# A gated linear recurrence with its key-times-query scores on the diagonal computed once for both directions, and matmul chunks of two projections moved

## The reference, cut to what matters

```
def hgrn2_mixer(h, w_in, lb, gn_g, w_out):
    q, z_f, z_b, v, g = jnp.split(h @ w_in, 5, axis=-1)
    q = jax.nn.silu(q.astype(jnp.float32))
    ...
    # q2, v2, z2: 8 heads forward and the same 8 heads with time reversed
    logf = jnp.logaddexp(jnp.log(lb_h), jnp.log1p(-lb_h) + jax.nn.log_sigmoid(z2))
    k2 = (1 - lb_h) * jax.nn.sigmoid(-z2)
    out = _chunk_scan(q2, logf, k2, v2)
    o = out[:, :, 0] + out[:, ::-1, 1]
    o = o * lax.rsqrt(jnp.mean(o * o, axis=-1, keepdims=True) + EPS)
    o = o * gn_g.astype(jnp.float32).reshape(HGRN_HEADS, HGRN_DV)
    o = o.reshape(b_sz, s_len, D_MODEL).astype(h.dtype) * jax.nn.silu(g)
    return o @ w_out
# in _chunk_scan, bcum being the running sum of logf in a chunk:
#   scores[t, s] = sum_k q[t, k] * exp(bcum[t, k] - bcum[s, k]) * k[s, k]   for s <= t
#   o = (q * exp(bcum)) @ state + scores @ v
```

## Time and profile before

| | us |
|---|---|
| median of 3 runs | 2232.5 (2225.56 to 2234.05) |
| the profiled execution | 2231.72 |
| its span | 2229.9 |
| PE busy | 2108.7 (95%) |
| DVE busy | 1484.1 (67%) |
| ACT busy | 917.9 (41%) |

### The profile page before, as it was taken

The page is one execution under the profiler, slowest core; times in us unless marked ns, Lnnn a source line. Parts: engine busy times, 40 slices in busy tenths (PEclk is TensorE's granted clock), DMA queues, the critical chain, the costliest instruction groups (busy, mean ns, idle before and its releaser), DMA issues.

```text
span 2229.9 us, 26958 instructions
## 1 busy us (share of the span) xinstructions
PE 2108.7 (95%) x10048; PEld 1637.4 (73%) x10048; DVE 1484.1 (67%) x2641; ACT 917.9 (41%) x1737; POOL 15.5 (1%) x15
## 2 busy tenths in 40 slices
PE   4888999999998999999999999999999989999998
PEld 2665567777666776577888887788888777888886
DVE  6567775667365599977565555899999965343433
ACT  3344453344443342344233233665666634232231
POOL 1000000000000000000000000000000000000000
PEclk8999998999998999999999999999999999999999
DMA  8422222343223221134555551111111112232321
GB/s 327 170 97 73 88 71 71 132 143 114 95 92 105 68 67 48 38 133 151 180 191 177 186 187 61 57 58 50 55 49 56 48 50 82 86 104 95 94 95 57
DMA packets 65985, 228.77 MB, mean 103 GB/s; under 512 B 7105, under 2 KB 9281, under 8 KB 65729
## 3 DMA queue, kind: packets, MB, share of 16 engines
q1 hardware_dynamic: 65856, 227.05, 30.6%
HBM read 224.93 MB, written 2.10 MB: 102 GB/s over the span
## 4 chain that ended last, share of the span: by engine, by line
PE 78%; DVE 14%; ACT 4%; issue 3%; DMA 1%; SPq 0%; DVEq 0%; ACTq 0%
PE bank L377 20%; PE bank L379 20%; PE bank L378 20%; DVE arena L1737 6%; PE bank L1999 4%; PE bank L649 2%; PE bank L683 1%; PE bank L1188 1%; PE bank L1213 1%; DVE w_lo L315 1%; PE bank L2036 1%; PE bank L1202 1%; DVE arena L497 1%; ACT arena L1231 1%; PE bank L933 1%
## 5 line engine op out<-in xcount | busy, mean ns | idle before, releaser
L377 PE MATMUL bank<-h_hi,w_hi 128*128 128x512 f32 (+1 forms) x1616 | 666.0, 412 | 24.8 <-DVE h_lo L643 13.2
L379 PE MATMUL bank<-h_hi,w_lo 128*128 128x512 f32 (+1 forms) x1616 | 638.3, 395 | 0.0
L378 PE MATMUL bank<-h_lo,w_hi 128*128 128x512 f32 (+1 forms) x1616 | 636.1, 394 | 0.0
L306 ACT ACTIVATE w_hi<-w_raw 128x1024 fp32r<-128x1024 f32 (+3 forms) x293 | 290.9, 994 | 300.0 <-PE bank L379 289.5
L315 DVE TENSOR_TENSOR w_lo<-w_raw,w_hi 128x1024 fp32r<-128x1024 f32 (+3 forms) x290 | 332.8, 1149 | 88.4 <-ACT w_hi L306 88.0
L377 PEld LDWEIGHTS bank<-h_hi,w_hi 128*128 128x128 f32 (+1 forms) x1616 | 307.8, 190 | 99.6 <-issue 28.7
L379 PEld LDWEIGHTS bank<-h_hi,w_lo 128*128 128x128 f32 (+1 forms) x1616 | 306.5, 190 | 68.6
L378 PEld LDWEIGHTS bank<-h_lo,w_hi 128*128 128x128 f32 (+1 forms) x1616 | 308.0, 191 | 61.2 <-issue 4.1
L377 PE MATMUL bank<-a_hi_t,w_hi 128*128 128x512 f32 x512 | 203.0, 396 | 0.0
L378 PE MATMUL bank<-a_lo_t,w_hi 128*128 128x512 f32 x512 | 203.0, 396 | 0.0
L379 PE MATMUL bank<-a_hi_t,w_lo 128*128 128x512 f32 x512 | 202.9, 396 | 0.0
(11 more groups left out here) (254 smaller groups left out, 2475.0 us busy)
## 6 DMA issues: line engine op xcount, KB each, us to landing
w_raw<-weights_dram SPq DMA_DIRECT2D x261, 512.0 KB, 3.6
ada_raw<-ada_dram SPq DMA_DIRECT2D x128, 512.0 KB, 3.6
arena<-ada_dram SPq DMA_DIRECT2D x8, 1024.0 KB, 15.8
w_raw<-weights_dram SPq DMA_DIRECT2D x16, 256.0 KB, 2.6
xT<-x_dram SPq DMA_DIRECT2D x1, 2048.0 KB, 14.4
out_dram<-xT SPq DMA_DIRECT2D x8, 256.0 KB, 2.2
tables<-tables_dram SPq DMA_DIRECT2D x1, 1536.0 KB, 19.8
w_raw<-weights_dram SPq DMA_DIRECT2D x8, 144.0 KB, 3.5
```

What stands on the lines that cost most here:

```text
L306: nc.scalar.activation(WH[:, slot, 0:w], RAW[:, raw, 0:w], ACT.Copy).then_inc(w_hi_ready, 1)
L377: nc.tensor.matmul(o, WH[:, slot, cols], self.hi(k), start=(k == 0), stop=False)
L378: nc.tensor.matmul(o, WH[:, slot, cols], self.lo(k), start=False, stop=False)
L379: last = nc.tensor.matmul(o, WL[:, slot, cols], self.hi(k), start=False, stop=(k == self.K - 1))
```

## The change

It does five things.

1. Own scores are shared: DVE adds the keys of both directions (`add_keys`, into `KK`) once per head, PE computes one own score per head, and DVE keeps its diagonal once. `A` is not begun anew for direction 1, and `pv_own` runs once per head, after both directions. So a head has 15 scores and not 16, and its counts of `pv` are 3 and not 4.
2. The score of level 64 (p = 1) is computed only where it is needed: 64 keys by 64 queries of each token tile, and DVE moves it by a plain copy of 64 partitions by 4x64.
3. The other levels' `pick` copies only the half of each block pair that the level can fill, 256 and not 512 elements per partition, still through the mask.
4. Unit 0 takes 4 of its 10 parts of the next projection in slot 0, ahead of the first cross product; each other slot has 1 part.
5. The output projection has three tiles in its chunk-by-chunk opening. Chunks 0 to 6 of the third are put into `HgrnEnd`: two behind `pv_own`, five behind `sum_pe`.

Besides, `R` takes the place of `SQ`, and the second norm's steps are renumbered for a projection with one step less.

```diff
             def score_pe(self, pe, u, p):
-                e = 8 * u + p
+                e, d = self.event(u, p), u % 2
                 if e >= 2:
                     pe.wait_ge(self.picked.sem, self.picked.at(e - 1))
                 if p == 0:
-                    pe.wait_ge(self.k_made.sem, self.k_made.at(u + 1))
+                    pe.wait_ge(self.k_added.sem, self.k_added.at(u // 2 + 1))
...
+                    if p == 1:
+                        keys, queries = 64 * d, 64 - 64 * d
+                        last = nc.tensor.matmul(bank[4 + e % 2][keys:keys + 64, j * P + queries:j * P + queries + 64], lhs[:, j * P + keys:j * P + keys + 64],
+                                                rhs[:, j * P + queries:j * P + queries + 64], start=True, stop=True)
...
+            def add_keys(self, dve, h):
...
+                nc.vector.tensor_tensor(self.KK, K[:, 0, :], K[:, 1, :], ALU.add).then_inc(self.k_added.sem, 1)
...
+                if p == 1:
+                    keys, queries = slice(64 * d, 64 * d + 64), slice(64 - 64 * d, 128 - 64 * d)
+                    nc.vector.tensor_copy(A3[keys, :, queries], b3[keys, :, queries]).then_inc(self.picked.sem, 1)
                 else:
...
+                    half = slice(m, 2 * m) if d == 0 else slice(0, m)
...
+                    nc.vector.copy_predicated(A4, mask.unsqueeze(1).to_broadcast([P, NT, P // (2 * m), m]), b4).then_inc(self.picked.sem, 1)
...
+                self.parts = self.PARTS if u else (4, 1, 1, 1, 1, 1, 1)
...
                 if l == 0:
-                    self.part(pe, 0)
-                    if u:
-                        H.pv_own(pe, u - 1)
-                    H.score_pe(pe, u, 0)
+                    for i in range(self.parts[0]):
+                        self.part(pe, i)
+                    if u == 0:
+                        H.cross_pe(pe, 0)
+                    if d == 0:
+                        if h:
+                            H.pv_own(pe, h - 1)
+                        H.score_pe(pe, u, 0)
                     H.score_pe(pe, u, 1)
...
             def pe(self, pe):
-                self.H.pv_own(pe, 15)
+                self.H.pv_own(pe, 7)
+                for k in range(2):
+                    self.project.chunk(pe, k, (2,))
                 self.H.sum_pe(pe, 7)
+                for k in range(2, 7):
+                    self.project.chunk(pe, k, (2,))
...
-            weave((pr, 2, 1), (gains, 2.1, 1), (n2, 3.2, 0.2, 0, 2), (n2, 4.2, 1, 2, 8), (n2, 10.3, 1, 8, 9))
+            weave((pr, 2, 1), (gains, 2.1, 1), (n2, 3.2, 0.2, 0, 3), (n2, 4.2, 1, 3, 8), (n2, 9.3, 1, 8, 9))
```

More of the change, by code:

```diff
@@ L1993, in score_pe @@
                     pe.wait_ge(self.ready.sem, self.ready.at(g + 1))
[L1994 removed]
+                    lhs = rhs = self.X[:, g % 2, :]
                 for j in range(NT):
                     c = slice(j * P, (j + 1) * P)
[L1997 to L1999 removed]
+                    if p == 1:
+                        keys, queries = 64 * d, 64 - 64 * d
+                        last = nc.tensor.matmul(bank[4 + e % 2][keys:keys + 64, j * P + queries:j * P + queries + 64], lhs[:, j * P + keys:j * P + keys + 64],
+                                                rhs[:, j * P + queries:j * P + queries + 64], start=True, stop=True)
+                    else:
+                        last = nc.tensor.matmul(bank[4 + e % 2][:, c], lhs[:, c], rhs[:, c], start=True, stop=True)
                 last.then_inc(self.scored.sem, 1)
             def pick(self, dve, u, p):
[L2003 removed]
+                e, d = self.event(u, p), u % 2
                 dve.wait_ge(self.scored.sem, self.scored.at(e + 1))
@@ L2038, in pv_cross, with pv_own @@
                 last.then_inc(self.pv.sem, 1)
-            def pv_own(self, pe, u):
-                h = u // 2
-                pe.wait_ge(self.picked.sem, self.picked.at(8 * u + 8))
-                for r in range(NT):
-                    last = nc.tensor.matmul(bank[6 + h % 2][:, self.tile(u, r)], self.VT[:, self.order(u, r), :], self.A[:, self.tile(u, r)],
-                                            start=False, stop=True, skip_group_check=True)
+            def pv_own(self, pe, h):
+                pe.wait_ge(self.picked.sem, self.picked.at(15 * h + 15))
+                for j in range(NT):
+                    c = slice(j * P, (j + 1) * P)
+                    last = nc.tensor.matmul(bank[6 + h % 2][:, c], self.VT[:, j, :], self.A[:, c], start=False, stop=True, skip_group_check=True)
                 last.then_inc(self.pv.sem, 1)
             def square_act(self, act, h):
-                act.wait_ge(self.pv.sem, self.pv.at(4 * h + 4))
+                act.wait_ge(self.pv.sem, self.pv.at(3 * h + 3))
                 if h:
-                    act.wait_ge(self.summed.sem, self.summed.at(h))
+                    act.wait_ge(self.applied.sem, self.applied.at(2 * h - 1))
                 nc.scalar.activation(self.SQ, bank[6 + h % 2][:], ACT.Square).then_inc(self.squared.sem, 1)
@@ L2088, in build, with chunk @@
         class Begun(Project):
-            def chunk(self, pe, k):
-                for t in range(self.outer):
+            def chunk(self, pe, k, tiles=(0, 1)):
+                for t in tiles:
                     if k == 0:
@@ L2102, in first_tiles @@
             def first_tiles(self, pe):
-                self.chunk(pe, self.K - 1)
+                self.chunk(pe, self.K - 1, range(self.outer))
         class Slot(Stage):
@@ L2130, in pe @@
                         H.tokens_pe(pe, h)
-                    self.part(pe, 1)
+                    for i in range(1, self.parts[1]):
+                        self.part(pe, i)
                 else:
                     H.score_pe(pe, u, l + 1)
-                    for i in range(self.PARTS[l]):
+                    for i in range(self.parts[l]):
                         self.part(pe, i)
@@ L2204, in dve @@
                         H.scan(dve, u + 1)
-                elif l == 1:
+                elif l == 1 and d == 0:
                     H.pick(dve, u, 0)
```

50 lines of the change are left out of this document (33 added, 17 removed).

## The result

The changed kernel takes 2216.0 us (median of 7 runs, 2211.57 to 2219.84), the one before 2234.05 in the same comparison; the ratio is 0.992, with an interval of 0.9908 to 0.9931. It is faster by 18 us, where I had forecast 27 or 28, and lies 1 us outside my range. The profiled execution took 2211.57 us.

A forecast was written before the change was run, and what follows sets the result against it. PE was taken to set the pace in heads 0 to 6. Gains of 13.3 (heads), 2.0 (unit 13), 3.6 (opening), 2.6 (head 7) and 6.1 (end) sum to 27.6 us, giving 2204.5 us, range 2199 to 2215.

The forecast's parts named there:

- What bounds the kernel: Heads 0 to 6: PE sets the pace, with DVE 3 us per head behind; in units 14 and 15 ACT and DVE.
- Scores and `pv_own`: Heads 1 to 6: one own score and one `pv_own` fewer per head, cheaper level-64 scores; 2.2 us per head, 13.3 us.
- The quads' part: Level-64 scores, two per head, as eight small matmuls: 0.67 us instead of 0.89, saving 0.22 us each.
- Does DVE allow it?: Slot 0 of direction 1 could pinch; DVE at 43.6 us per head beside PE's 48.3, so PE just not held up.
- The half picks: DVE's half-size predicated copies take 265 ns off 732; 12 picks save 3.2 us per head.
- The added wait of `pv_own` for pick 7: Slot 0: added keys, 0.6 us on DVE, precede the pick `pv_own` waits for; 2.7 us of PE work hides it.
- Opening: Unit 0: four parts fill the 5.34 us gap before the first cross product, then DVE paces; 3.6 us gained.
- The end: Last `pv_own` to the second norm: third-tile matmuls fill the gap, 37.0 us instead of 43.15; 6.1 us gained.
- Head 7: Units 14 and 15: earlier own pick, copy and smaller picks on DVE save 0.6 and 2.0, together 2.6 us.
- DVE takes over: Rival: halved copies cost as much as whole, slot 0 of direction 1 holds PE; gain 18 us, 2214; chance 0.09.
- The small scores dearer: Rival: small level-64 scores save nothing or cost; some 6 us less gain, 2210.5; chance 0.12.
- the opposite rival: Predicated copies over short runs slower than whole rows, deciding from 1.12 us a pick; about 2260 at 1.3; chance 0.04.

The follow-up runs named there:

- e9_long_runs: Changed kernel with the half picks of levels 2 and 1 copying one run of 64 elements (wrong output); head 49.46 us, ratio 0.9914 to the kernel before.
- e5_no_opening: Changed kernel with unit 0's projection parts put back as before, the cross product ahead of them; stage 443.31 us, ratio 0.9928 to the kernel before.
- e12_clock: Order of e7_act_order plus unread filler matmuls in the waits of units 14 and 15; 2212.0 us, ratio 0.9903 to the kernel before.
- e7_act_order: Changed kernel with ACT's key gate and sigmoid, and DVE's sigmoid product, one slot later in direction 1; head 48.95 us, ratio 0.9915 to the kernel before.

## Why the prediction was right or wrong

- **What bounds the kernel**: right at the start, PE without waits in heads 0 to 6, but the reading was too coarse. "PE sets the pace and DVE stands 3 us per head behind" is a sum over a head; the limit that came next was a chain across ACT and DVE, 22 us long from a sum in direction 0 to a score in direction 1.
- **Scores and `pv_own`, 13.3 us**: the work did go. Before, the `pv_own` and two scores in direction 1 with the entry and the exit of the stretch took 3.15 us by starts, now the one small event takes 1.28, 1.87 less where I had 2.0. The quads' part was too large, 0.08 instead of 0.22 for each: the whole event in that place costs 0.81, since the 0.89 is the price behind another small set of matmuls. That is some 2 us of the miss over seven heads.
- **"Does DVE allow it?" is the step that failed.** I wrote "By my walk PE is just not held up" and walked DVE's own instructions in slot 0 of direction 1, with a lead of 1.5 us. What was missing is ACT: DVE's L1879 in slot 1 waits for the sigmoid that ACT makes behind three exponentials and a gate, which all begin with DVE's L1893. That wait costs PE 0.79 us at the level-16 score. The other 0.25 us by which direction 1's 23.72 exceed the 22.68 that the removed work would give are, by starts, small delays and longer records of the scores of levels 32, 16 and 8. Against before, a head gained 1.1 us on the average (0.94 against the usual 50.57; one head of before took 50.87) and not 2.2.
- **The half picks**: 265 ns off was right or better for eight of twelve (0.43 us against my 0.47) and wrong for the four of levels 2 and 1, which save nothing. My row for it was `mult`, a multiplication that doesn't slow down on such runs (mean 416 ns over all levels). By `e9_long_runs` it costs the kernel 0.17 us a head.
- **The added wait of `pv_own` for pick 7**, costed at nothing: it shows no wait in heads 1 to 6.
- **Opening, 3.6**: 3.3 in the change, 2.9 of it by `e5_no_opening`, with DVE as the pace. **The end, 6.1**: 5.9; the last chunk began 7.75 us behind `pv_own` (7.74 predicted).
- **Head 7, 2.6**: unit 15 gave 1.5. Unit 14 lost 1.1, because the clock fell ahead of the waiting score and not behind its start, and the root stood behind half-rate matmuls. I had thought of the clock at the two ends only, not at the wait inside unit 14, which was there before (3.68 us, now 3.87). Why it fell earlier stays open. `e12_clock` gives both units 2.1 us against before, near the 2.6.
- **The rivals**: "DVE takes over" had the right place (a PE wait for `mult` in the early slots of direction 1) and its total of 18 us is what was measured, but it named the wrong cause: the level is 16, not 32, and cheaper picks didn't remove the wait. That its total fits is in part luck, as its 2.5 for the opening was too low and its 1.2 for head 7 too high. I gave it 0.09. "The small scores dearer" was part of it. A predicated copy over short runs is slower than over long ones, as the opposite rival said, but at 0.73 us it costs a whole one's price and far less than the 1.12 from which that rival would decide.

The terms, in us: heads 6.7 short, unit 13 1.2, head 7 2.2, opening 0.3, end 0.2; together 10.6 of the 27.6.

What stays open: with no wait of PE for another engine in the timeline of `e7_act_order`'s heads, direction 1 takes 23.02 us where the work removed would give 22.68. By starts that 0.34 lies at two scores, of levels 32 and 8, which begin some 0.05 and 0.14 us later than at a matmul's distance and then last 0.89 instead of 0.81; I did not try to remove that. And why the clock falls at one wait and not at another of nearly that length isn't settled; only that it stayed up in the run with both filled.

## What to carry to other kernels

When work is taken from the engine that paces, look at each stretch from which it goes, and follow the profile's chain through all other engines, from the point where it leaves the pacing engine to the next hand-over: what the busy shares leave free over a whole head may not be free there. Compare the pacing engine's own work between these points with the length of the chain beside it (here 21.5 us against 22.3, and 23.2 with the sharing undone). In this case reordering the queue of an engine in the chain mended it, and saving work on DVE hardly did. Where TensorE has waits of some microseconds, look at the clock behind each of them: here the time was won only with both filled.

## What the runs showed of the hardware

- A predicated copy of 256 fp32 elements per partition takes 0.43 us in runs of 4 to 32 elements or of 64, and 0.73 us in runs of 2 and 1, as much as one of 512 whole (0.732); packing the mask changes nothing. A multiplication in the same seven shapes has a mean of 0.416 us.
- Eight 64x64 matmul records take 0.61 us by starts, and the first starts 0.33 us behind a 128x512 matmul instead of 0.23. The Trainium skill, page TensorEngine Tiling (Array Packing), section Tiling Modes, Key Properties, has a change of tiling mode drain TensorE. The trace agrees in that there is a price, 0.10 us in and 0.02 out, and shows it far below a whole matmul's length of 0.39.
- With waits of 3.87 and 1.80 us filled by matmuls the granted clock stayed at 1.00 through head 7. With only the first filled it fell at the second, with neither it fell at the first alone (the changed kernel) or at both (`e7_act_order`). The Trainium skill, page TensorE: Matmul & The Clock Gate, section Part 1, says that the gate follows how busy TensorE has been, and the runs agree in so far as filling kept it up; they don't show why it fell at a wait of 1.80 us in one run and not in another.
